# ScalarE begins the convolution's two PSUM accumulators in place of VectorE

## The reference, cut to what matters

```
def _odd_mixer(h, w_in, conv_w, conv_b, ln_g, ln_b, w_out):
    proj = jnp.einsum('bsd,de->bse', h, w_in)
    val, gt, z = proj[..., :C], proj[..., C:2*C], proj[..., 2*C:]
    g = val * jax.nn.sigmoid(gt)
    c = depthwise causal convolution of g along positions, 31 taps per channel
    c = c + conv_b
    mu = mean(c, channels); cc = c - mu; var = mean(cc * cc, channels)
    c = cc * rsqrt(var + LN_EPS) * ln_g + ln_b
    y = silu(c) * silu(z)
    return einsum('bse,ed->bsd', y, w_out)
```

## Time and profile before

| | us |
|---|---|
| median of 3 runs | 1587.95 (1586.36 to 1589.12) |
| the profiled execution | 1586.52 |
| its span, first to last instruction | 1583.3 |
| granted TensorE clock, mean | 0.984 of full speed |
| convolution with its projections | about 1346 to 1508 in the span |

### The profile page before, as it was taken

The page is one execution under the profiler, slowest core; times in us unless marked ns, Lnnn a source line. Parts: engine busy times, 40 slices in busy tenths (PEclk is TensorE's granted clock), DMA queues, the critical chain, the costliest instruction groups (busy, mean ns, idle before and its releaser), DMA issues. The chain is left out here.

```text
span 1583.3 us, 18928 instructions
## 1 busy us (share of the span) xinstructions
PE 1475.1 (93%) x6999; PEld 1163.3 (73%) x6999; DVE 880.2 (56%) x1249; ACT 606.3 (38%) x912; POOL 383.1 (24%) x494
## 2 busy tenths in 40 slices
PE   3799999999899999898999999999899999989977
PEld 2688888888678777466888888888677787767555
DVE  5676525533463666846443344432665557799964
ACT  3422212322342453753442212231631245776634
POOL 3011101000000000021004888400202100899900
PEclk9799999999999999999999999999999999999979
DMA  9687635333224122014323433453133223222201
GB/s 347 204 267 262 237 94 159 120 106 98 81 76 129 53 67 75 5 23 105 106 85 102 133 117 97 146 219 95 54 94 110 78 83 93 80 67 81 67 27 53
DMA packets 204708, 177.91 MB, mean 112 GB/s; under 512 B 7379, under 2 KB 184079, under 8 KB 204118
## 3 DMA queue, kind: packets, MB, share of 16 engines
q1 hardware_dynamic: 188438, 121.87, 26.1%
q0 software_dynamic: 15040, 52.89, 9.5%
q10 hardware_dynamic: 1152, 2.10, 0.3%
HBM read 168.37 MB, written 8.46 MB: 112 GB/s over the span
## 5 line engine op out<-in xcount | busy, mean ns | idle before, releaser
L1986 PE MATMUL ps<-h_hi,w_hi 128*128 128x512 f32 x1224 | 491.2, 401 | 31.0 <-DVE h_lo L1281 18.1
L1988 PE MATMUL ps<-h_hi,w_lo 128*128 128x512 f32 x1224 | 479.3, 392 | 0.0
L1987 PE MATMUL ps<-h_lo,w_hi 128*128 128x512 f32 x1224 | 479.0, 391 | 0.0
L1241 DVE TENSOR_TENSOR w_lo<-w_stage,w_hi 128x1024 fp32r<-128x1024 f32 x225 | 294.6, 1322 | 234.1 <-ACT w_hi L782 231.6
L782 ACT ACTIVATE w_hi<-w_stage 128x1024 fp32r<-128x1024 f32 x225 | 230.7, 1048 | 199.5 <-PE ps L1988 187.6
L1986 PEld LDWEIGHTS ps<-h_hi,w_hi 128*128 128x128 f32 x1224 | 231.2, 189 | 101.4 <-issue 51.1
L1987 PEld LDWEIGHTS ps<-h_lo,w_hi 128*128 128x128 f32 x1224 | 231.3, 189 | 48.9 <-issue 3.1
L1988 PEld LDWEIGHTS ps<-h_hi,w_lo 128*128 128x128 f32 x1224 | 230.9, 189 | 49.4
L1986 PE MATMUL ps<-a_hi,w_hi 128*128 128x512 f32 x544 | 214.3, 394 | 13.1 <-DVE a_lo L1922 9.4
L1988 PE MATMUL ps<-a_hi,w_lo 128*128 128x512 f32 x544 | 212.8, 391 | 0.0
L1987 PE MATMUL ps<-a_lo,w_hi 128*128 128x512 f32 x544 | 212.7, 391 | 0.0
(11 more groups left out here) (423 smaller groups left out, 1458.4 us busy)
## 6 DMA issues: line engine op xcount, KB each, us to landing
w_stage<-in_w_gu SPq DMA_DIRECT2D x88, 512.0 KB, 4.3
ada_w<-in_w_ada POOLq DMA_DIRECT2D x72, 512.0 KB, 6.4
w_stage<-in_w_down SPq DMA_DIRECT2D x44, 512.0 KB, 3.7
w_stage<-in_w_in SPq DMA_DIRECT2D x24, 512.0 KB, 3.8
w_stage<-in_odd_w_in SPq DMA_DIRECT2D x24, 512.0 KB, 3.7
w_stage<-in_even_w_in SPq DMA_DIRECT2D x16, 512.0 KB, 3.8
w_stage<-in_w_out SPq DMA_DIRECT2D x8, 512.0 KB, 3.7
mats<-mats_d POOLq DMA_DIRECT2D x4, 1024.0 KB, 7.9
```

The lines of the kernel that those rows point to most:

```text
L1241: dve.tensor_tensor(w_lo[:, c % RING], w_in[:, c % RING], w_hi[:, c % RING].bitcast(F32), ALU.subtract).then_inc(w_split, 1)
L1986: pe.matmul(bank, w_hi[:, slot, k], rhs_hi, start=start, stop=False, skip_group_check=True)
L1987: pe.matmul(bank, w_hi[:, slot, k], rhs_lo, start=False, stop=False, skip_group_check=True)
L1988: return pe.matmul(bank, w_lo[:, slot, k], rhs_hi, start=False, stop=stop, skip_group_check=True)
```

## The change

`ACT_TAPS` gives ScalarE two taps in tiles 0 and 1 and one in the others, so VectorE keeps 15, 15, 16, 16, 16, 16, 10, 12: 116 taps, each now adding to a bank. A new function `begin(t)` on ScalarE writes both banks. It stands in step n % 3 = 0 between `hi` and the tanh, for t = n // 3 - 1, and for the last tile behind its tap number 5. At n = 9 the copy to `m0n` is put ahead of it. VectorE waits for `begun` before a tile's first tap and before it writes `gb` again. Some semaphores elsewhere are merged to free a name.

```diff
 POOL_TAPS = [13] * 6 + [11, 8]
-DVE_TAPS = [TAPS - 1 - p - q for p, q in zip(POOL_TAPS, PE_TAPS)]
+ACT_TAPS = [2, 2] + [1] * 6
+DVE_TAPS = [TAPS - 1 - p - q - r for p, q, r in zip(POOL_TAPS, PE_TAPS, ACT_TAPS)]
...
                     t = n // 3
+                    if n == 9:
+                        act.wait_ge(mean_sum, 1)
+                        act.activation(m0n[:], ps[6][:], ACT.Copy, scale=-1.0 / P).then_inc(m0_ready, 1)
+                    if n % 3 == 0:
+                        begin(t - 1)
                     if n % 3 == 0:
                         upto(act, g_ready, t - 1)
                         act.activation(tmp[:, t % 2], ps[n % 4][:], ACT.Tanh, scale=0.5).then_inc(odd_read, 1)
...
-                for k in range(4, POOL_TAPS[KT - 1]):
+                for k in range(4, 6):
+                    tap(KT - 1, k)
+                begin(KT - 1)
+                for k in range(6, POOL_TAPS[KT - 1]):
                     tap(KT - 1, k)
...
+            def begin(t):
+
+                act.wait_ge(g_ready, t + 1)
+                upto(act, cv_ready, t)
+                k = TAPS - DVE_TAPS[t] - ACT_TAPS[t]
+                if t < 2:
+                    act.activation(ps[4][:], gb[:, t % 2, k:k + S], ACT.Copy, scale=cw[:, t, k:k + 1])
+                else:
+                    act.wait_ge(m0_ready, 1)
+                    act.activation(ps[4][:], m0n[:], ACT.Copy)
+                k += ACT_TAPS[t] - 1
+                act.activation(ps[5][:], gb[:, t % 2, k:k + S], ACT.Copy, scale=cw[:, t, k:k + 1]).then_inc(begun, 1)
...
                     dve.wait_ge(g_ready, t + 1)
+                    if third == 0:
+                        dve.wait_ge(begun, t + 1)
                     for k in range(first + third * DVE_TAPS[t] // 3, first + (third + 1) * DVE_TAPS[t] // 3):
                         acc = ps[4 + (k - first) % 2][:]
                         upto(dve, tap_done, base + (k - first) - 1)
-                        if k < first + 2:
-                            upto(dve, cv_ready, t)
-                        if k == first and t >= 2:
-                            dve.wait_ge(m0_ready, 1)
-                            dve.scalar_tensor_tensor(acc, gb[:, t % 2, k:k + S], cw[:, t, k:k + 1], m0n[:],
-                                                     ALU.mult, ALU.add).then_inc(tap_done, 1)
-                        elif k < first + 2:
-                            dve.tensor_scalar(acc, gb[:, t % 2, k:k + S], cw[:, t, k:k + 1], None, ALU.mult) \
-                                .then_inc(tap_done, 1)
-                        else:
-                            dve.scalar_tensor_tensor(acc, gb[:, t % 2, k:k + S], cw[:, t, k:k + 1], acc,
-                                                     ALU.mult, ALU.add).then_inc(tap_done, 1)
+                        dve.scalar_tensor_tensor(acc, gb[:, t % 2, k:k + S], cw[:, t, k:k + 1], acc,
+                                                 ALU.mult, ALU.add).then_inc(tap_done, 1)
...
                         upto(dve, tap_prod, of_tiles(POOL_TAPS, t - 1))
+                        upto(dve, begun, t - 1)
```

More of the change, by code:

```diff
@@ L378, in build_program @@
         hn_ready, h_hi_ready, h_ready = sem("hn_ready"), sem("h_hi_ready"), sem("h_ready")
+        begun = sem("begun")
         silu_ready, prod_ready, a_hi_ready, a_ready = sem("silu_ready"), sem("prod_ready"), sem("a_hi_ready"), sem("a_ready")
@@ L390, in build_program @@
         v_t, v_done = sem("v_t"), sem("v_done")
-        mo_done = sem("mo_done")
         nm_stored, bm_in = sem("nm_stored"), [sem("bm_in0"), sem("bm_in1")]
@@ L396, in build_program @@
         head_t, hy_ready, mix_hi, mix_ready = sem("head_t"), sem("hy_ready"), sem("mix_hi"), sem("mix_ready")
-        lnc_in, s_ready, s_max, s_exp, p_norm = sem("lnc_in"), sem("s_ready"), sem("s_max"), sem("s_exp"), sem("p_norm")
+        s_ready, s_max, s_exp, p_norm = sem("s_ready"), sem("s_max"), sem("s_exp"), sem("p_norm")
         pt_t, pt_ready, pv_ready = sem("pt_t"), sem("pt_ready"), sem("pv_ready")
@@ L403, in build_program @@
         mats_in = [[sem("b_in0"), sem("b_in1")], [sem("c_in0"), sem("c_in1")]]
-        pool_in, pads_zero = sem("pool_in"), sem("pads_zero")
+        pool_in, edges_zero = sem("pool_in"), sem("edges_zero")
         even_read, ut_done, ut_ready, uc_done, uc_ready = (sem("even_read"), sem("ut_done"), sem("ut_ready"),
@@ L412, in build_program @@
                                                          sem("glu_read"), sem("gp_ready"))
-        cw_in, cw_t, cw_ready, odd_zero = sem("cw_in"), sem("cw_t"), sem("cw_ready"), sem("odd_zero")
+        cw_in, cw_t, cw_ready = sem("cw_in"), sem("cw_t"), sem("cw_ready")
         tap_ready, g_ready, odd_read, pool_tap = sem("tap_ready"), sem("g_ready"), sem("odd_read"), sem("pool_tap")
@@ L561, in _ @@
             pool.wait_ge(qk_done, 8)
-            pool.dma_start(ln_count[:], a["ln_count"]).then_inc(lnc_in, 16)
+            pool.dma_start(ln_count[:], a["ln_count"]).then_inc(mix_const, 16)
             def set_up():
@@ L743, in even_mixer @@
                 pool.memset(pads[:, :, 0:16], 0.0)
-                pool.memset(pv[:, :, 0:16], 0.0).then_inc(pads_zero, 1)
-                pool.wait_ge(pads_zero, 1)
+                pool.memset(pv[:, :, 0:16], 0.0).then_inc(edges_zero, 1)
+                pool.wait_ge(edges_zero, 1)
                 pool.wait_ge(pool_in, 32)
@@ L759, in odd_mixer @@
                 pool.memset(ln_eps[:], 1e-5)
-                pool.memset(gb[:, :, 0:TAPS - 1], 0.0).then_inc(odd_zero, 1)
+                pool.memset(gb[:, :, 0:TAPS - 1], 0.0).then_inc(edges_zero, 1)
                 for t in range(KT):
@@ L1137, in odd_mixer @@
                         first_tap(t)
-                    if n == 9:
-                        act.wait_ge(mean_sum, 1)
-                        act.activation(m0n[:], ps[6][:], ACT.Copy, scale=-1.0 / P).then_inc(m0_ready, 1)
                     for u in range(KT - 2):
@@ L1226, in _ @@
             chain = [0]
+            mo_done = [0] * MH
             def link(ins):
@@ L1405, in project_posts @@
                         dve.wait_ge(proj_read, n - 1)
-                        dve.tensor_scalar(mo[:, h], mo[:, h], 0.5, 0.5, ALU.mult, ALU.add).then_inc(mo_done, 1)
+                        dve.tensor_scalar(mo[:, h], mo[:, h], 0.5, 0.5, ALU.mult, ALU.add).then_inc(dve_self, 1)
+                        chain[0] += 1
+                        mo_done[h] = chain[0]
                     if n == 1:
@@ L1555, in head_out @@
                 dve.wait_ge(head_t, h + 1)
-                dve.wait_ge(mo_done, h + 1)
+                dve.wait_ge(dve_self, mo_done[h])
                 dve.scalar_tensor_tensor(mo[:, h], ps[7 if h else 2][:], cols[:, G_MH + h:G_MH + h + 1], mo[:, h],
@@ L1569, in attention @@
                         if q == 0:
-                            dve.wait_ge(lnc_in, 16)
+                            dve.wait_ge(mix_const, 7 * 16)
                         if q == 2:
@@ L1738, in take @@
                     elif n < 12:
-                        dve.wait_ge(pads_zero, 1)
+                        dve.wait_ge(edges_zero, 1)
                         dst = pv[:, (n - 5) // 2 % 2, 16:]
@@ L1828, in odd_mixer @@
                 dve.wait_ge(cw_ready, 1)
-                dve.wait_ge(odd_zero, 1)
+                dve.wait_ge(edges_zero, 2)
                 def taps(t, third):
@@ L2360, in outputs @@
                     if t == 0:
-                        pe.wait_ge(pads_zero, 1)
+                        pe.wait_ge(edges_zero, 1)
                     of_toep = mats[:, t % 2, 2].rearrange("p (l g h) -> p l g h", l=L, g=8)
```

## The result

| | before | after |
|---|---|---|
| median over 12 runs each, us | 1585.82 (1581.39 to 1589.12) | 1591.70 (1589.48 to 1597.26) |
| after over before | | 1.0044, interval 1.0029 to 1.0058 |
| profiled execution, its span | 1586.52, 1583.3 | 1597.07, 1594.7 |
| the stage (below), us | 162.79 | 168.67 |

What follows compares the result with a forecast made beforehand. GpSimd was taken as the bound; +4.1 us up to TensorE's last wait and +1.25 in the last tile made +5.4, from 1587.95 to 1593.3 us. The range was 1585.3 to 1596.5, reaching to the first rival.

Steps and rivals of the forecast that it cites:

- The sum for the range: Whole run: write costs between two ends give 5.4 - 1.2 to 5.4 + 2.2; with scatter of 1.4, 1590.5 to 1596.5.
- The bound: In the stage's tiles: GpSimd never rests and sets the pace; VectorE's 11.4 us of removed work becomes idle time.
- Rival 2: In the stage: VectorE was the bound, so 11.4 us less, 1576.5 us; chance 7%.
- The eaten lead: Border of two tiles: begin's wait and writes use up the 3.4 us lead of product 4; GpSimd starves 1.24 us.
- The sum by tiles: Up to TensorE's last wait: n = 6 +1.33, n = 9 +0.05, n = 12, 15, 18 +0.91 each, together +4.1 us.
- the term of the hand-over: Border of two tiles: from the merge's end on VectorE to begin on ScalarE, taken as 0.04 us.
- The last tile: Tile 7: VectorE's wait for begin costs 1.95 us and gives back one tap; last merge +1.25 us.
- The price of a write into PSUM: ScalarE's begin: 0.52 us a write without a scale, 0.61 with one; 1.22 in tiles 0 and 1, 1.13 after.
- the two ends I gave: ScalarE's begin: bounds of 0.48 and 0.72 us a write, so 0.96 and 1.44 over two writes.
- the 1.2 us that I worked out by it: Seven begins: if ScalarE reaches PSUM faster than SBUF, 0.17 less in each, some 1.2 us.
- The first rival: Tile borders: begin is hidden and GpSimd, freed of waits for VectorE's m0n taps, gains 2.3 us: 1585.7; chance 15%.
- third rival: In the stage: late w_lo waits one more add, +6.9 us on top, 1600; or TensorE's idling lowers its clock; chance 8%.

Runs made afterwards that it cites:

- e7: Kernel before, without ten taps of the convolution and without adding m0n on VectorE (another result is computed): stage 3.42 us shorter.
- e12: Kernel before, with GpSimd given 12 taps instead of 13 in tiles 0 to 5 and VectorE 18 there: stage 155.89 us, whole runs 0.45% under before.
- e1: Changed kernel, with begin moved from ahead of the tanh to behind products 4 and 5, the last tile's left in place: stage 161.20 us.
- e3: Changed kernel, with only the tanh moved ahead of begin: stage 3.26 us under the changed kernel.
- e4: Changed kernel, with two more 128x512 copies behind those of begin, into an unused part of a_hi: stage 6.46 us over the changed kernel.
- e5: Kernel before, with only ScalarE's wait for the previous tile's merge added at begin's place, nothing written: stage 0.44 us longer.
- e6: Kernel before, with only sixteen more ScalarE copies at begin's place, into an unused part of a_hi, without the wait: stage 0.01 us longer.
- e9: Kernel before, with both the wait for the merge and the sixteen copies on ScalarE at begin's place: stage 6.83 us longer.
- e2: e1 with the last tile begun by VectorE as before: stage 159.67 us.
- e11: Changed kernel, with begin moved behind all of the step's products (after number 8): stage 164.32 us.

## Why the prediction was right, step by step

**The numbers.** Forecast were +5.4 and 1593.3 us, measured are +5.88 in the stage and 1591.70. The sum for the range is slightly off: 1587.95 + 5.4 + 2.2 + 1.4 is 1596.95, not 1596.5, and nothing hangs on it. Nor is VectorE the busier of the two, as the text reads the page's slices: in the earlier trace rows GpSimd is, with 19.71 against 19.40.

**The bound.** That GpSimd and not VectorE sets the pace is shown by e7 (3.4 us of 11.4) and by e12 (a tap more on VectorE, 6.9 us less). Rival 2 would have the opposite in both.

**The eaten lead.** Shown by e1, e3, e4 and the trio e5, e6, e9. GpSimd starves 1.45 us a border, 1.37 beyond the usual gap of 0.08, where the prediction had 1.24. The missing 0.13 is the hand-over from VectorE to ScalarE: I took 0.04, and the trace has 1447.24 to 1447.41, 0.17. `begin` was 1.15 for my 1.13.

**The sum by tiles.** From the distances of the g writes, after less before: n = 6 +1.41 (forecast 1.33), n = 9 -0.10 (+0.05), n = 12, 15, 18 +1.04, +1.01, +1.05 (0.91 each), together 4.41 for 4.1. So the term of the hand-over is the one that was short. At n = 9 two terms of opposite sign were off by a little: product 4 was taken 0.75 later for 0.69, and the freed port gave back 0.85 for 0.64.

**The last tile.** +1.47 (5.88 - 4.41) for 1.25. Of it, 1.04 is the border n = 21, where GpSimd starves 1.47 us once more, and only 0.43 arises behind tile 7's write of `gb`. ScalarE and VectorE of the changed kernel, against the earlier trace rows:

```profile
1502.98 0.60 ACT L1142 ACTIVATE zo<-ps 128x512 f32<-128x512 f32 x1 [3.57 <-PE ps L2003]
...
1507.72 0.72 ACT L1209 ACTIVATE sq<-gb,cw 128x512 f32<-128x512 f32 x1 [0.38 <-POOL pacc L767]
1508.35 0.58 ACT L1195 ACTIVATE ps<-m0n 128x512 f32<-128x512 f32 x1
1508.87 0.67 ACT L1197 ACTIVATE ps<-gb,cw 128x512 f32<-128x512 f32 x1
...
1509.63 8.00 DVE L1863 SCALAR_TENSOR_TENSOR ps<-gb,cw,ps 128x512 f32<-128x512 f32 x12 [2.60 <-ACT ps L1197]
```

The merge of tile 6 is over at 1507.03; VectorE then idles 2.60 us, because ScalarE makes product 5 first and that waits for GpSimd. With the begin of this tile alone undone, e2 is 1.53 under e1. As forecast, TensorE hides ScalarE's own delay of n = 21 (the silu still waits 3.57 us for it), and what GpSimd lost there is passed on to product 5 and to VectorE, as the prediction's 1.25 has it.

**The price of a write into PSUM.** Durations of 0.58 to 0.60 without and 0.67 to 0.68 with a scale, a few hundredths under those into SBUF (0.61 and 0.71 in e6), but from start to start 0.53 and 0.61 to 0.62, the same as there. So of the two ends I gave, the middle held. The Trainium skill's rule that ScalarE reaches PSUM faster (ScalarE: Activation LUTs, Step-by-step: what each stage is for) holds for the duration here and gave nothing in a row of writes; the 1.2 us that I worked out by it did not come.

**The port.** The first rival's mechanism is real and was paid: GpSimd's add at the border is 1.30, and tiles without the `m0n` taps are 20.44 instead of 20.77. It wasn't enough where the lead was gone. e1 is that rival come true, -1.6 us.

**The clock.** In the tile shown above the granted clock was 1.00 as before, but the third rival's second half did occur twice in this stage. TensorE at its last wait, and the stretch that follows (columns as in the earlier trace rows):

```profile
1476.93 0.47 PE L2001 MATMUL ps<-h_hi,w_hi 128*128 128x512 f32 x1 [2.50 <-DVE w_lo L1261]
...
1477.60:1481.01 3.41, 3.41 (x10) 2.63 (x9) 3.08 (x5) 2.40 (x4) 3.17 (x4) 0.50 0.57 159
```

The granted clock stood at 0.50, the level of 1.2 GHz, for 3.4 us from 1477.60, behind a wait of 2.50 us, and matmuls started 0.43 apart in place of 0.23. The same happened from 1433.23, around the end of a wait of 2.48 us. An earlier wait of 2.56 us was followed by no fall, so what decides it was not shown. In the kernel before, e1 and e3 the clock is 1.00 from the start of the stage to 1500. From TensorE's last wait to the silu of tile 7 it was 24.4 us before and is 26.05 now, so the second fall cost TensorE 1.6 us. Nearly all of it went into the time that ScalarE had to spare: from tile 7's write of `gb` to the last merge this kernel takes 21.35 and e1 and e3, without a fall, 21.13. So about 0.2 us of the 5.88 is the clock's by this estimate, a term that the prediction's sum doesn't have; the first half of that rival, +6.9 by a `w_lo` that comes late, did not come.

## What to carry to other kernels

Ahead of moving work to a less busy engine, ask what stands behind it in that engine's order: a short instruction that waits for a far producer holds up everything behind it, and a wait and a piece of work that are each covered by the same slack are not covered together. Put such an instruction behind those that feed the bound, at a place where the engine waits for the bound anyway. And find the bound by taking work out or shifting one unit of it: here VectorE, at 93% busy, had room for one tap more a tile, while GpSimd at 95% had none. The work that was moved here was worth 3.4 us at most, for 11.4 us less of VectorE's time.

## What the runs showed of the hardware that I had not expected

Busy time is no measure of an engine's room where engines exclude each other at a port. The three `w_lo` of a tile on VectorE took 1.69, 2.08 and 2.14 us in e1, where two of them followed a wait for `w_hi`. They took 1.21 to 1.33 in e11 and 1.21, 1.77 and 1.88 in e12, where VectorE came late to them. The short ones are unexpected, since GpSimd was as dense there. In these traces the duration of `w_lo` goes with when VectorE reaches it; why a late `w_lo` hardly waits in e11 was not shown.

A delay on another engine can also come back as TensorE's clock. The changed kernel has three waits of TensorE for `w_lo` of about 2.5 us in the stage, where the kernel before has none over 1.7, and at two of them the granted clock fell to 0.50 for 3.4 us.
